# RWKV-7 scan inside a hybrid diffusion backbone: backward chunk matrices in the other partition halves, next step's operands one level later, state scaling on GpSimd

## The reference, cut to what matters

```python
def step(S, inp):
    rt, wt, kt, vt, at, bt = inp
    sa = jnp.einsum('bhvk,bhk->bhv', S, at)
    S = S * wt[:, :, None, :] + sa[..., None] * bt[:, :, None, :] + vt[..., None] * kt[:, :, None, :]
    return S, jnp.einsum('bhvk,bhk->bhv', S, rt)
```

## Time and profile before

| what | value |
|---|---|
| median of 3 runs | 2470.89 us (2470.61 to 2472.47) |
| the profiled execution | 2470.64 us |
| its span, first to last instruction | 2468.7 us |
| PE busy | 2196.2 us, 89% of the span |
| DVE, ACT, POOL busy | 745.4, 510.6 and 287.7 us |
| mean granted TensorE clock | 0.954 |

### The profile page before, as it was taken

How to read it: one execution, slowest core, us unless ns; L and a number is a source line. 1 busy time by engine, 2 the same in 40 slices (tenths; PEclk the granted TensorE clock), 3 DMA queues, 4 the chain that set the end, 5 groups by cost and what they waited for, 6 DMA issues and landing times. The chain is left out here.

```text
span 2468.7 us, 58810 instructions
## 1 busy us (share of the span) xinstructions
PE 2196.2 (89%) x26490; PEld 1414.7 (57%) x26490; DVE 745.4 (30%) x1642; ACT 510.6 (21%) x1122; POOL 287.7 (12%) x461
## 2 busy tenths in 40 slices
PE   6989999899899999999999698998999899977774
PEld 2434443798844444446566464555898688744443
DVE  1023334766531011310100122456676311300002
ACT  2022322333230000301111132323332301200001
POOL 0000000433200000001111200002443000011111
PEclk9999999899999999999999889998999899998887
DMA  7139816000032222348999811110000344899993
GB/s 273 69 109 330 315 46 230 3 4 4 10 104 78 70 83 103 145 173 314 381 385 385 311 47 45 62 47 2 4 4 4 137 153 154 284 338 384 379 384 132
DMA packets 182934, 400.23 MB, mean 162 GB/s; under 512 B 6656, under 2 KB 29952, under 8 KB 182496
## 3 DMA queue, kind: packets, MB, share of 16 engines
q1 hardware_dynamic: 170528, 361.94, 40.8%
q0 software_dynamic: 8576, 23.08, 2.5%
q10 hardware_dynamic: 3648, 12.45, 1.7%
HBM read 365.47 MB, written 31.98 MB: 161 GB/s over the span
## 5 line engine op out<-in xcount | busy, mean ns | idle before, releaser
L472 PE MATMUL ps<-H,memory 128*128 128x512 f32 (+2 forms) x1728 | 618.3, 515 | 11.9 <-DMA memory<-in_w_in 10.1
L472 PEld LDWEIGHTS ps<-H,memory 128*128 128x128 f32 (+1 forms) x1728 | 330.1, 192 | 287.9 <-issue 251.3
L707 PE MATMUL ps<-memory 64*64 64x64 f32 (+1 forms) x12672 | 384.2, 223 | 40.5 <-issue 16.2
L707 PEld LDWEIGHTS ps<-memory 64*64 64x64 f32 x12672 | 364.9, 136 | 56.1 <-issue 34.4
L965 PE MATMUL ps<-memory 128*32 128x256 f32 x5120 | 306.6, 402 | 59.0 <-DMA memory<-in_eu 57.4
L472 PE MATMUL ps<-memory 128*128 128x512 f32 (+4 forms) x960 | 339.7, 504 | 17.1 <-DVE memory L1431 10.6
L965 PEld LDWEIGHTS ps<-memory 128*32 128x32 f32 x5120 | 193.2, 116 | 170.2 <-issue 91.2
L472 PEld LDWEIGHTS ps<-memory 128*128 128x128 f32 (+2 forms) x960 | 176.7, 186 | 170.4 <-issue 142.2
L1872 POOL TENSOR_TENSOR memory<-memory,cons 128x256 f32<-128x256 f32 x160 | 128.0, 813 | 192.3 <-DVE memory L1560 139.1
L990 PE MATMUL ps<-memory 128*32 128x256 f32 x2560 | 144.8, 380 | 4.9 <-ACT memory L1311 3.8
L1936 POOL DMA_DIRECT2D expert_rows<-memory x128 | 69.3, 541 | 437.0 <-DVE memory L1807 416.1
(11 more groups left out here) (251 smaller groups left out, 1792.8 us busy)
## 6 DMA issues: line engine op xcount, KB each, us to landing
memory<-in_eg SPq DMA_DIRECT2D x32, 2048.0 KB, 19.0
memory<-in_eu SPq DMA_DIRECT2D x32, 2048.0 KB, 24.9
memory<-in_ed SPq DMA_DIRECT2D x32, 2048.0 KB, 21.6
memory<-in_w_ada SPq DMA_DIRECT2D x24, 2048.0 KB, 10.3
memory<-in_w_in SPq DMA_DIRECT2D x20, 2048.0 KB, 9.1
expert_rows<-memory SPq DMA_DIRECT2D x4, 3456.0 KB, 23.7
memory<-in_w_out SPq DMA_DIRECT2D x4, 2048.0 KB, 8.5
memory<-expert_rows ACTq DMA_DIRECT2D x19, 384.0 KB, 7.0
```

Of the source, the lines that this page charges most:

```text
L472: ins = mm(ps[0:M, bank, 0:w], lhs(k), rhs(k), start=(k == 0), stop=(k == n - 1))
L707: ins = mm(out[cols, j], lhs[rows, j, :], rhs[rows, j], start=(n == 0), stop=(n == len(terms) - 1))
```

## The change

Seven edits, all in the scan but the last:

1. Backward (d = 1) products of `turns`, `readout`, `update`, part of `grams` and a second copy of the values (`Vx`) are made or held in exchanged halves, and both directions are interleaved product by product. `solve` makes its d = 1 result exchanged too: its entry goes from (1, 0) to (1, 1). `values` grows from 16 products to 24, and grams from 32 to 40 (`last_gram` is 8 of them, after `solve`); ACT has one more copy.
2. `readout` of both directions stands in level 1, `update` of both in level 2. The d = 1 readout is made in two parts, so `read` has two adds for d = 1. `update` writes where a readout part was and waits for both `read`.
3. ACT's exponentials of step k+1 move from levels 0 and 1 to 1 and 2; DVE's `totals` and `operands` from levels 1 and 2 to 2 and 3; both `read` stand after level 1.
4. DVE's state add stands after the operands in levels 2 and 3, and its scaling becomes `carry` on GpSimd, ahead of `queries` in levels 3 and 4. `values` waits for the scaled state as before.
5. The backward cumulation is one scan over reversed columns in the place of a scan and two operations.
6. The two masks of the d = 1 grams for the readout become one operation of 512 columns.
7. At the start, PE waits for all 8 squares before the first of its 8 sums, in the place of one wait for each.

```diff
-                 "Vt": [[quads(raw[d][:, 512 * p:512 * p + 256]) for d in range(2)] for p in range(2)],
+                 "Vt": [[quads(raw[0][:, 512 * p:512 * p + 256]), quads(VB[p][:, 0:256])] for p in range(2)],
+                 "Vx": [[quads(raw[0][:, 512 * p:512 * p + 256]), quads(VB[p][:, 256:512])] for p in range(2)],
...
+                    pe.wait_ge(sem("squares"), KD)
                     for k in range(KD):
-                        pe.wait_ge(sem(f"squares{k % 2}"), k // 2 + 1)
...
+                    v = [V[:, :, columns(k, d)] for d in both]
+                    heads(None, (part(1, 0, 0), (v[1], eye, 0, 0)))
+                    heads("values", (part(0, 0, 0), (v[0], eye, 0, 0)), (part(1, 1, 0), (v[1], eye, 0, 1)))
...
-                    pe.wait_ge(sem("values_held"), nth(N, d))
-                    if k >= 2 and streams(l, k - 2):
-                        pe.wait_ge(sem("read"), 2 * readouts(l, k - 2) - 1 + d)
-                    if streams(l, k):
-                        pe.wait_ge(sem("queries"), 2 * readouts(l, k) - 1 + d)
-                        heads(None, (part(d, 0, 1), (ONCE["bE2"][d], TWICE["Rq"][p][d], 0, 0)))
-                    heads("grams", (ps[:, 4 * d + 1, 0:256 * wide].rearrange("p (x j n) -> p j x n", x=wide, n=CH),
-                                    (ONCE["bKk"][d], ER[p][d][:, 0:wide].rearrange("p x j n -> p j x n"), 0, 0)))
+                    left = (ps[:, 1, 0:256 * wide].rearrange("p (x j n) -> p j x n", x=wide, n=CH),
+                            (ONCE["bKk"][0], ER[p][0][:, 0:wide].rearrange("p x j n -> p j x n"), 0, 0))
+                    if not streams(l, k):
+                        heads("grams", left)
+                        return
+                    heads(None, (part(0, 0, 1), (ONCE["bE2"][0], TWICE["Rq"][p][0], 0, 0)),
+                          (part(1, 1, 0), (ONCE["bE2"][1], TWICE["Rq"][p][1], 0, 1)))
+                    heads("grams", left, (part(1, 1, 1), (ONCE["bKk"][1], TWICE["Rq"][p][1], 0, 1), None))
+                def last_gram(k):
+                    heads("grams", (part(1, 0, 1), (ONCE["bKk"][1], TWICE["E3"][k % 2][1], 0, 0)))
                 def turns(k):
                     for d in both:
                         if k:
                             pe.wait_ge(sem("u_copied"), nth(l * STEPS + k - 1, d))
-                        heads(None, (part(d, 3, 0), (ONCE["bE2"][d], eye, 0, 0)))
-                        heads("turns", (part(d, 3, 1), (ONCE["bKk"][d], eye, 0, 0)))
+                    heads(None, *((part(d, 3, 0), (ONCE["bE2"][d], eye, 0, d)) for d in both))
+                    heads("turns", *((part(d, 3, 1), (ONCE["bKk"][d], eye, 0, d)) for d in both))
...
-                    heads("u", *((part(d, 3, 1), (TWICE["XT"][p][d], ONCE["RHS"][d], d, 0)) for d in both))
-                def readout(k, d):
+                    heads("u", *((part(d, 3, 1), (TWICE["XT"][p][d], ONCE["RHS"][d], d, d)) for d in both))
+                def readout(k):
                     N, p = l * STEPS + k, k % 2
-                    pe.wait_ge(sem("u_copied"), nth(N, d))
-                    if k + 1 < STEPS:
+                    for d in both:
+                        pe.wait_ge(sem("u_copied"), nth(N, d))
+                        if k + 1 < STEPS:
+                            pe.wait_ge(sem("masked"), nth(N + 1, d))
+                    own = [((ONCE["U"][d], TWICE["Grb"][p][d], d, 0), (TWICE["Vx"][p][d], TWICE["Grk"][p][d], d, 0)) for d in both]
+                    past = [(ONCE["S"][d], TWICE["Rq"][p][d], 0, 0) for d in both]
+                    heads("readout", (part(0, 1, 0), *own[0], past[0]), (part(1, 1, 0), *own[1], None),
+                          (part(1, 0, 0), None, None, past[1]))
+                def update(k):
+                    N, p = l * STEPS + k, k % 2
+                    for d in both:
+                        pe.wait_ge(sem("u_copied"), nth(N, d))
                         pe.wait_ge(sem("masked"), nth(N + 1, d))
-                    heads("readout", (part(d, 1, 0), (ONCE["S"][d], TWICE["Rq"][p][d], 0, 0),
-                                      (ONCE["U"][d], TWICE["Grb"][p][d], 0, 0), (TWICE["Vt"][p][d], TWICE["Grk"][p][d], 0, 0)))
-                def update(k, d):
-                    N, p = l * STEPS + k, k % 2
-                    pe.wait_ge(sem("u_copied"), nth(N, d))
-                    pe.wait_ge(sem("masked"), nth(N + 1, d))
-                    heads("step", (part(d, 0, 0), (TWICE["Bt"][p][d], ONCE["U"][d], 0, 0),
-                                   (TWICE["Kt"][p][d], TWICE["Vt"][p][d], 0, 0)))
+                        if streams(l, k):
+                            pe.wait_ge(sem("read"), 2 * readouts(l, k) - 1 + d)
+                    heads("step", *((part(d, 0, 0), (TWICE["Bt"][p][d], ONCE["U"][d], d, 0),
+                                     (TWICE["Kt"][p][d], TWICE["Vx"][p][d], d, 0)) for d in both))
...
-                    grams(k, 0)
+                    grams(k)
                     if k:
                         solve(k - 1)
-                    grams(k, 1)
+                    last_gram(k)
                     if more:
                         turns(k)
                     for n in range(len(LEVELS)):
                         join(k, n, 0)
-                        if k and n < 2 and streams(l, k - 1):
-                            readout(k - 1, n)
-                        if k and 2 <= n < 4:
-                            update(k - 1, n - 2)
+                        if k and n == 1 and streams(l, k - 1):
+                            readout(k - 1)
+                        if k and n == 2:
+                            update(k - 1)
...
+                            act.copy(flat(TWICE["Vt"][k % 2][1]), part(1, 0, 0))
+                            act.copy(flat(TWICE["Vx"][k % 2][1]), part(1, 1, 0)).then_inc(sem("values_held"), 1)
...
-                        if more and n < 2:
-                            decays(k + 1, n)
-                            decays_before(k + 1, n)
-                            growths(k + 1, n)
+                        if more and n in (1, 2):
+                            decays(k + 1, n - 1)
+                            decays_before(k + 1, n - 1)
+                            growths(k + 1, n - 1)
...
-                        link(dve.tensor_tensor_scan(flat(first), con_("reset", RJ * CH), flat(lw), 0.0,
-                                                    ALU.mult, ALU.add))
-                        link(tt(L, lw, first, ALU.subtract))
-                        tt(L, L, first[:, :, CH - 1:CH].broadcast_to([P, RJ, CH]), ALU.add)\
-                            .then_inc(sem("cumulated"), 1)
+                        dve.tensor_tensor_scan(flat(L)[:, ::-1], con_("reset", RJ * CH), flat(lw)[:, ::-1], 0.0,
+                                               ALU.mult, ALU.add).then_inc(sem("cumulated"), 1)
...
                         link(tt(y, y, half(d, 1, 0), ALU.add))
+                        if d:
+                            link(tt(y, y, half(1, 0, 0), ALU.add))
                         dve.nop().then_inc(sem("read"), 1)
...
-                    link(tt(state, state, half(d, 0, 0), ALU.add))
-                    tt(state, state, total[:, k % 3, d, :].unsqueeze(2).broadcast_to([P, RJ, CH]), ALU.mult)\
-                        .then_inc(sem("state"), 1)
+                    tt(state, state, half(d, 0, 0), ALU.add).then_inc(sem("stepped"), 1)
...
-                        if n in (1, 2):
-                            if more:
-                                totals(k + 1, n - 1)
-                                operands(k + 1, n - 1)
-                            if k:
-                                read(k - 1, n - 1)
-                        if k and n == 3:
+                        if k and n == 1:
                             for d in range(2):
-                                update(k - 1, d)
+                                read(k - 1, d)
+                        if more and n in (2, 3):
+                            totals(k + 1, n - 2)
+                            operands(k + 1, n - 2)
+                        if k and n in (2, 3):
+                            update(k - 1, n - 2)
...
+                def carry(k, d):
+                    state = ONCE["S"][d]
+                    pool.wait_ge(sem("stepped"), carried(l, k, d))
+                    tt(state, state, total[:, k % 3, d, :].unsqueeze(2).broadcast_to([P, RJ, CH]), ALU.mult)\
+                        .then_inc(sem("state"), 1)
...
+                        if k and n >= 3:
+                            carry(k - 1, n - 3)
                         if more and n >= 3:
                             queries(k + 1, n - 3)
```

54 lines of the change are left out of this document (35 added, 19 removed).

## The result

| | median | runs |
|---|---|---|
| before | 2470.75 us | 2470.18 to 2472.47, 4 runs |
| changed | 2495.41 us | 2492.77 to 2503.17, 4 runs |

The ratio is 1.0105, with a 95% interval of 1.0085 to 1.0126: 24.7 us more, where 24.5 were forecast. The profiled execution of the changed kernel took 2492.77 us, its span is 2491.1, so it is 22.1 above the profiled one of before, at the same mean granted clock (0.956 for 0.954). It is also the fastest of the four runs of the changed kernel, so what its trace shows is the low end of the slowdown.

What follows compares the result with a forecast made beforehand. PE looked like the limit, with the level chain and code loading behind it. Eight full steps +18.5, second layer +4, steps 7 +1.8, steps 0 -2, scan ends +0.8, squares +1.4: +24.5 on 2470.9, 2495 us; range 2478 to 2512.

Runs made afterwards that it cites:

- e9: Kernel before with one product of couple and one of grams merged in 12 steps, 8 fewer of 464: 2470.7 us against 2473.64, ratio 0.999.
- e5: The changed kernel's exchanged halves and mixed directions on a schedule close to that of the kernel before: 2483.53 us, ratio 1.0054 to before.
- e4: Changed kernel with DVE's reads ahead of level 1's adds and its state add before the operands: 2481.42 us, ratio 1.0029 to before.
- e6: Kernel before with the 32 mixed products of couple issued twice in each of 16 steps: 2495.1 us, ratio 1.0095.
- the repeat: Changed kernel traced again, unaltered, as the 128 idle instructions meant for it were not in the built program: 2500.24 us, one run.
- e3: Changed kernel with DVE's state add ahead of totals and operands in levels 2 and 3: 2498.82 us, ratio 1.0102 to before.
- e1: Changed kernel with both reads ahead of level 1's adds on DVE: 2487.65 us, ratio 1.0053 to before.

## What to carry to other kernels

Where PE runs thousands of small products, count its instructions as well as its time: a wait without a releaser that comes back every 126 matmul records, where each has its own weight load as here, is code, and an edit that halves issue time but not the list meets it. Before pricing an engine's lost wait, ask what its time was hiding; here stalls of 17 us were worth between 4 and 13. Look at the granted clock of each stretch before two traces are subtracted; one drop cost about 2 us here, as much as several of the effects sought. And trace the changed kernel more than once. To shorten such a list, merge products that share a left operand, and put on an engine's list first what another engine waits for, but price what then stands last.

## What the chip showed that was not expected

- PE took blocks of code no faster than some 4.0 us each in the mean of a full step in five lists of 456 to 496 products (e9 28.9 / 7.2 = 4.0, before 29.3 / 7.4 = 3.96, e5 3.98, e4 30.7 / 7.64 = 4.02, e6 31.1 / 7.9 = 3.9), while busy time ranged from 25.8 to 28.6 us. Between waited-for blocks with no other wait between them single distances ran from 3.4 to 4.8 us. A block's packet starts only when PE has begun the block before it, and PE goes on 2.1 to 2.9 us behind the packet's start; why these vary is open.
- Idle products ahead of the scan moved its long code waits by 63 records each, and a wait is not of one length: the two of 0.58 and 1.06 at records 825 and 951 were 1.18 and 1.33 in the repeat, and with the list shifted the first was 1.61 and the second 0.18.
- One of DVE's operand products takes 0.95 us in before, and 0.41 where GpSimd is idle. The changed kernel has its L1575 at 0.41 too, since GpSimd waits for the state add then; in e3 it is 0.84. It saves nothing in the whole: in e3, where this order is given up, the time is the same, and in e4 less than in e1.
